# A two-layer hybrid decoder on one core: one input projection for prompt and samples, and a tile's expert choice moved to the next stretch

## The reference

```python
mod = (silu(c) @ w_ada + b_ada)                    # 6 x 1024 columns: shifts, gains, gates
h = rms_norm(x, norm1_g) * (1 + sc1) + sh1
qa, ka, va, qb, kb, vb, zb, bb, ab, qc, kc, vc = split_cols(h @ w_in, IN_SPLITS)   # 3592 columns
...                                                # three mixers: dilated windows, gated delta, sticks
x = x + gt1 * (concat([o_a, o_b, o_c]) @ w_out)
h2 = rms_norm(x, norm2_g) * (1 + sc2) + sh2
x = x + gt2 * peer_ffn(h2, peer_wq, peer_keys, peer_u, peer_v)
```

## The kernel before

| stretch | us in the trace | prompt lane | sample lane | experts |
|---|---|---|---|---|
| A | 22 to 54 | 4 chunks of modulation, layer 0 | - | - |
| B | 56 to 992 | unit 0, with layer 1's modulation beside its two choices | layer 0, with the other 8 chunks of layer 0's modulation between `heads` and `delta_sample` | - |
| C | 992 to 1931 | unit 1 | - | samples of layer 0; unit 0 |
| D | 1936 to 2780 | unit 2 | - | unit 1 |
| E | 2784 to 3638 | unit 3 | - | unit 2 |
| F | 3643 to 4684 | - | layer 1 | unit 3; samples of layer 1 |

## Time and profile before

### The profile page before, as it was taken

How to read it: one execution, slowest core, us unless ns; L and a number is a source line. 1 busy time by engine, 2 the same in 40 slices (tenths; PEclk the granted TensorE clock), 3 DMA queues, 4 the chain that set the end, 5 groups by cost and what they waited for, 6 DMA issues and landing times. The chain is left out here.

```text
span 4692.3 us, 42307 instructions
## 1 busy us (share of the span) xinstructions
PE 3425.7 (73%) x11982; PEld 1910.2 (41%) x11982; DVE 2843.8 (61%) x5777; ACT 877.2 (19%) x2045; POOL 2587.5 (55%) x2244
## 2 busy tenths in 40 slices
PE   5966768539298889575887967498898436748897
PEld 2624543126154554262455426255553113213351
DVE  1225552556866648787774688868649767584322
ACT  1113110011142112112321211242221011000120
POOL 0000362025767757687774667777656767665563
PEclk8986789759589999796998988799999767869896
DMA  6451375549989989899998889999988989999995
GB/s 229 139 180 56 101 227 177 187 104 320 354 318 345 385 308 339 331 399 342 366 376 320 306 334 395 353 346 361 367 306 308 378 303 348 362 382 377 336 330 154
DMA packets 586674, 1401.71 MB, mean 299 GB/s; under 512 B 67314, under 2 KB 287659, under 8 KB 585244
## 3 DMA queue, kind: packets, MB, share of 16 engines
q0 software_dynamic: 306176, 1107.44, 63.6%
q1 hardware_dynamic: 261836, 274.77, 17.7%
q10 hardware_dynamic: 18432, 16.79, 1.1%
HBM read 1387.11 MB, written 11.88 MB: 298 GB/s over the span
## 5 line engine op out<-in xcount | busy, mean ns | idle before, releaser
L2496 PE MATMUL bank<-arena 128*128 128x512 f32 (+1 forms) x3264 | 1589.6, 636 | 200.5 <-PEq L2493 117.9
L2392 POOL DMA_INDIRECT arena<-in_peer_u_dram,arena x1056 | 1279.6, 1212 | 693.2 <-issue 303.1
L2392 POOL DMA_INDIRECT arena<-in_peer_v_dram,arena x1056 | 1160.5, 1099 | 749.2 <-PE bank L2496 448.4
L2442 DVE CUSTOM_DVE_ANT_0 arena<-arena 128x1024 f32<-128x1024 f32 (+1 forms) x1056 | 1269.8, 1224 | 447.5 <-DMA arena<-in_peer_u_dram,arena 417.4
L2496 PEld LDWEIGHTS bank<-arena 128*128 128x128 f32 (+1 forms) x3264 | 614.8, 196 | 1013.6 <-issue 869.5
L2479 ACT ACTIVATE arena<-arena 128x128 f32<-128x128 f32 (+1 forms) x816 | 301.5, 394 | 1072.9 <-PE bank L2496 686.1
L2458 DVE SCALAR_TENSOR_TENSOR arena<-arena 128x1024 f32<-128x1024 f32 x232 | 297.6, 1283 | 243.6 <-DMA arena<-in_peer_v_dram,arena 223.3
L799 PE MATMUL bank<-arena 128*128 128x256 f32 (+3 forms) x1472 | 368.9, 414 | 101.0 <-PEq L792 95.9
L2138 POOL DMA_INDIRECT arena<-in_cache_sb_k_dram,arena x64 | 84.0, 1312 | 550.4 <-POOLq L2131 530.2
L799 PEld LDWEIGHTS bank<-arena 128*128 128x128 f32 (+1 forms) x1472 | 247.0, 170 | 220.8 <-issue 156.1
L641 PE MATMUL bank<-arena 128*9 128x512 f32 x384 | 180.3, 627 | 66.9 <-PEq L637 45.9
(11 more groups left out here) (339 smaller groups left out, 3730.0 us busy)
## 6 DMA issues: line engine op xcount, KB each, us to landing
arena<-in_w_in_dram SPq DMA_DIRECT2D x78, 1024.0 KB, 13.2
arena<-in_w_ada_dram SPq DMA_DIRECT2D x24, 2048.0 KB, 8.4
arena<-in_w_out_dram SPq DMA_DIRECT2D x24, 1024.0 KB, 13.0
arena<-in_peer_wq_dram SPq DMA_DIRECT2D x24, 1024.0 KB, 15.0
arena<-in_peer_u_dram,arena POOLq DMA_INDIRECT x1056, 7.4
arena<-in_peer_v_dram,arena POOLq DMA_INDIRECT x1056, 6.2
arena<-in_cache_sb_k_dram SPq DMA_DIRECT2D x128, 128.0 KB
arena<-in_cache_sb_v_dram SPq DMA_DIRECT2D x128, 128.0 KB
```

The costliest lines, as they stand in the source:

```text
L2392: pool_.indirect_dma_start(G_[g % GR][0:b.parts, :], None, tables[0 if which == "u" else 1], bass.IndirectOffsetOnAxis(ap=b.index[:, n:n + ...
L2442: vec.tensor_tensor_reduce(row, row, b.h, 1.0, 0.0, ALU.mult, ALU.add, b.AV[0:b.parts, n:n + 1]).then_inc(freed_by_dve, 1)
L2496: last = pe_.matmul(ps[6 + i][0:b.rows, :], DG[owners[g][1] % NDG][0:b.parts, 0:b.rows], G_[g % GR][0:b.parts, i * GBLK:(i + 1) * GBLK], s ...
```

## The change

1. **One projection for both lanes.** In stretches B and E `project` also takes the 8 samples of that layer: their normed rows stand as 8 more columns of `HT`, so a feature matmul has 264 columns, and each of the other eight chunks gets one more group of 8 matmuls (`"sample"`). The sample units' own norm, `project` and loads of `w_in` are gone; `sample_norm` runs ahead of the projection (in E as a stage of the prompt lane). In E the sample's rows go through three staging buffers to DRAM (`ROWS`), and `rows_back` reads them at F's start. `delta_sample` gets features (`BF`) and transposes them back for `DB`.
2. **Order in B.** The sample lane begins with its norm, then the 8 chunks of modulation (0.02 to 0.25 of the stretch, beside the projection), then waits for the prompt's projection (`after_lane`) and goes on.
3. **Choice.** B's prompt lane ends with unit 0's first choice, with all 12 chunks of layer 1's modulation beside it (length 80 where the two choices had 59 each). The choice of unit 0's second tile runs in C, from 0 to 0.25 of it (`second_choice`).
4. **Stores of modulation.** SP no longer waits for a store; DVE does, two chunks later.
5. **Last phase v.** In F, phase v of tile b alone puts every second row on DVE (`ON_DVE_ALONE = 2`).
6. F's sample lane has 0 to 0.8 of the stretch (before 0.85).

```diff
 def on_dve(b, n):
-    return not b.sample and n >= FIRST_ON_DVE and n % ON_DVE == ON_DVE - 1
+    return not b.sample and n >= FIRST_ON_DVE and n % b.every == b.every - 1
...
-                                    sp_.dma_start(MODD[l][:, cols(n - 2)], MT[n % 2]).then_inc(stored, 16)
-                                    sp_.wait_ge(stored, 16).then_inc(stored, -16)
+                                    sp_.dma_start(MODD[l][:, cols(n - 2)], MT[n % 2]).then_inc(v_landed[n % 2], 16)
...
+                            if n >= 2:
+                                vec.wait_ge(v_landed[n % 2], 16).then_inc(v_landed[n % 2], -16)
...
-            def project(u, m):
+            def project(u, m, s=None):
...
-                        mine = [(c, kind, i) for i in range(nt)]
+                        mine = [(c, kind, i) for i in range(nt)] + ([(c, kind, "sample")] if s else [])
...
+                        if spill and t - 2 in of_samples:
+                            k = of_samples.index(t - 2)
+                            lo, hi, _ = CHUNKS[groups[t - 2][0]]
+                            sp_.wait_ge(act2sp, 1).then_inc(act2sp, -1)
+                            sp_.dma_start(ROWS[:, lo:hi], s.m.STAGE[k % 3][:, 0:hi - lo]).then_inc(k_landed[k % 3], 16)
...
+                                elif i == "sample":
+                                    last = pe_.matmul(ps[t % BANKS][0:NB, 0:hi - lo], m.HT[:, k, n_:wide],
+                                                      m.W[c % ring][:, k, 0:hi - lo], start=(k == 0), stop=(k == KD - 1))
...
+                                if out_to_dram and k >= 3:
+                                    act_.wait_ge(k_landed[k % 3], 16).then_inc(k_landed[k % 3], -16)
...
-                    return [paced(begin, 8), paced(project(u, m), 80), paced(heads(u, m), 14)] + between + [paced(delta_sample(u, m), 75),
+                    return [paced(heads(u, m), 14), paced(delta_sample(u, m), 80),
...
+                before = [paced(sample_norm(s.u, m, m.HT), 8)] if s is not None and s.normed is None else []
+                return before + [paced(begin, 14), paced(project(u, m, s), 120 if s else 102), ...
...
-                        paced(choose_tile(u, e, 0, meanwhile[0:1]), 59), paced(choose_tile(u, e, 1, meanwhile[1:2]), 59)]
+                        paced(choose_tile(u, e, 0, meanwhile), 80 if meanwhile else 59)] + \
+                       ([] if meanwhile else [paced(choose_tile(u, e, 1), 59)])
...
+                        b.every = ON_DVE_ALONE if last and len(phase) == 1 else ON_DVE
...
+        def second_choice(u, span):
+
+            ticks, programs = LC.choose_tile(u, None, 1)
+            return [span[0] + (span[1] - span[0]) * (n + 1) / ticks for n in range(ticks)], programs
...
-        late = [LP.modulate(1, tiles, GBLK, half * MOD // 2, (half + 1) * MOD // 2) for half in range(2)]
+        late = [LP.modulate(1, tiles, GBLK)]
...
+               [([paced(LS.sample_norm(samples[0], rooms[0][0], m.HT), 8)], 0.0, 0.02), ([paced(rest, 50)], 0.02, 0.25), (rest_of_samples, 0.255, 1.0)], [])
...
+            choice = second_choice(u, (0.0, 0.25)) if k == 0 else ([], {})
...
-                window([], LS.token_mixers(samples[1], (LAST_at, arena_cols)), phases + [[("u", s)], [("v", s)]], (0.0, 0.85))
+                of_sample = [paced(LS.rows_back(samples[1], rooms[1][0]), 4)] + LS.token_mixers(samples[1], rooms[1])
+                window([], [(of_sample, 0.0, 0.8)], phases + [[("u", s)], [("v", s)]], choice)
```

More of the change, by code:

```diff
@@ L745, in project @@
                 tap = {i: f for f, i in feature_at.items()}
-                BANKS = 2 if u.sample else 4
+                of_samples = [i for i, g in enumerate(groups) if g[2] == "sample"]
+                spill = s is not None and s.m.STAGE is not None
+                BANKS = 4
                 ring = len(m.W)
                 ticks = len(groups) + 3
-                T = None if u.sample else m.TMP
+                T = m.TMP
                 def destinations(g):
@@ L834, in dve @@
                     for t in range(ticks):
-                        if t == 0 and not u.sample:
+                        if t == 0:
                             if u.first:
@@ L1875, in dve @@
                 def dve():
-                    for t in range(ticks):
+                    for t in range(-ahead, ticks):
                         if t == 2:
@@ L2346, in build, with experts @@
             batches = 0
[L2349 removed]
+        def experts(phases, last=False):
             walked = []
```

164 lines of the change are left out of this document (114 added, 50 removed).

## The result

The changed kernel takes **4643.28 us** (median of 4 runs, 4635.06 to 4653.99) where the kernel before took 4711.81 in the same comparison: ratio 0.9856, 95% interval 0.9827 to 0.9885, some 68 us saved where 103 were forecast. A second comparison on another chip gave 0.9859 (0.9836 to 0.9883).

| us | before | forecast | after | difference |
|---|---|---|---|---|
| B | 936 | -55 | 890 | -46 |
| C | 944 | +28 | 976 | +32 |
| D | 848 | 0 | 844 | -4 |
| E | 859 | +6 | 893 | +34 |
| F | 1041 | -82 | 966 | -75 |

A forecast was written before the change was run, and what follows sets the result against it. B was held to be bound by chains of waits, C, E and F by bytes and gathers in flight. Terms -55 (B), +28 (C), +6 (E), -82 (F) summed to -103, from median 4713.41 to 4610 us; range 4500 to 4685.

The forecast's parts named there:

- B, -55 forecast: Stretch B: projection and modulation -25, middle +20, end -50 us; bounds carried 0 and -110.
- -25, +20, -50: B's parts: fewer matmul records; samples' stick stage put ahead of the first choice; end keeping only samples' tail and modulation.
- the bound of 60: B's middle: samples' stick stage moved ahead of the first choice adds at most 60 us; +20 taken.
- C, +28 forecast: Stretch C: moved choice of 60 us, 18 hidden, 42 between tile a's dots, 14 absorbed; bounds 0 and +60.
- rival 2: C and F's third phase: POOL cannot issue gathers while DVE works beside them; C loses 60 us; 4667 us; chance 0.04.
- E, +6 forecast: Stretch E: samples' norm and 128 records join the first phase, whose length gathers set; bounds 0 and +44 us.
- F, -82 forecast: Stretch F: first phase -55, second +13, third -40 us; bounds -17 and -109.
- Rival 1: B: samples' chain of 659 us, as long and begun as late as before, keeps B's length; 4665 us; chance 0.17.
- Rival 3: E: ACT waits five times for stores to `ROWS` behind loads of `w_in`, 228 us; 4832 us; chance 0.05.
- Rival 4: Whole kernel, all goes well: B -110, C and E 0, F -109; 4494 us; chance 0.11.
- Rival 5: C: the choice comes late, tile b's gathers wait on POOL, C pays 35 us more; 4645 us; chance 0.06.

The follow-up runs named there:

- the square: Four kernels by projections and choice's place; B: 936 us before, 926 choice alone moved to C, 932 changed kernel with choice back in B, 890 both.
- e7_no_sample_groups: Changed kernel, E without the samples' eight row groups, their copies and stores; F reads rows of w_in instead: 4638.83 us, ratio 0.9838 to the kernel before.
- e11_f_samples_later: Changed kernel, F's sample lane from 0.07 to 0.9 of the stretch instead of 0 to 0.8: 4626.87 us, ratio 0.9826 to the kernel before.
- e4_b_samples_sooner: Changed kernel, B's sample lane behind the projection ends at 0.92 of the stretch instead of 1.0: 4632.86 us, ratio 0.9833 to the kernel before.
- e10_choice_first: Changed kernel, moved choice from 0 to 0.05 of C instead of 0 to 0.25: 4638.14 us, ratio 0.9864 to the kernel before.

## Why the prediction was right, and where it was wrong

The direction held, and the time lies in the range. Made against the profiled executions, the sum forecast 4591 and the profile shows 4635, 44 us less saved: E makes 28 of them, B 9, F 7, C 4, and D gives 4 back. That it came within the range is in part luck: inside B and F the terms missed by more than the sums, in both directions.

*B, -55 forecast, -46 measured.* By parts -25, +20, -50 came out as -30, +43, -59, so the middle was sized too small: the part ahead of the first choice grew by 43, well on the way to the bound of 60, and the end gave more. By the square the middle's 43 us go with the moved choice alone: with the choice back in B the first choice stood 31 us ahead of its old place, about as far as the beginning had become shorter. And the parts were added as if each had a price of its own. That holds up to the first choice; but the end became 27 us longer with the projection and 53 shorter with the choice, and 59 shorter with both. So one projection saves 4 us of B, and the choice 10. The working was near for the sum of the two and would have been far off for either.

*C, +28 forecast, +32 measured* (30 to 32 of it before tile a's last dot). The path is in the main the one that the step named, gathers that wait for buffers which the dots free; that the gathers themselves take longer (rival 2, below) it left out. The choice is 52 us of DVE here, not 60; 37 of them fell between the dots, where the step had 42, and they cost 32, nearly all, where the step let free time take a third. The step took its place in C as given; 0.1 instead of 0.25 makes it 11 to 18.

*E, +6 forecast, +34 measured: the step that failed.* It said that the gathers set the length, since PE had free time. The sample groups cost 9 to 13 us all the same (`e7_no_sample_groups`), though PE is busy for 61% of that phase: the gathers waited 20.0 us for the dots, and 3.4 without the groups. The longer lengths cost 6 us in the third phase and give them back in the first. Some 10 us of the second phase stay open: it lies at 401 to 425 us after, at 400 and 410 in the two profiles with E's code of before, and no run tells these apart. By the same two profiles E before is 859 and 872 us, so that of the +34 some 21 to 34 are the kernel's.

*F, -82 forecast, -75 measured*, but each phase otherwise: -18 for -55, -26 for +13, and up to the tail -30 between the marks used here, where -40 was forecast. The first phase lost the loads of `w_in` and took up other loads and 29 us of DVE; the step counted what goes and not what moves up when the sample lane has a stage less. The third gave some 10 us for the rows on DVE, and the other 20 otherwise: the step set the gathers' pace at 1.28 us, from 50 us at 401 GB/s; with PE waiting for rows the phase ran at a DMA share of 0.98 and 358 GB/s, 201/128 = 1.57 us a gather. The sum came within 7 us because misses of 37, 39 and 10 us cancel. That F's phases share the same bytes may be why (`e11_f_samples_later` moved 26 us from one to another), but it is argued and not shown, and no run gives the samples their own projection back in F.

**The rivals.** Rival 1, the samples' chain: it took 945.3 - 295.8 = 649 us, nearly the old 659, and B became shorter by about as much as the chain began earlier. That looked like it, and `e4_b_samples_sooner` speaks against it: the chain ended 50 us sooner, and B was as long. Nor is its length fixed: 599 us there, 686 with the choice back in B.

Rival 2, POOL held by DVE, would by its size have cost C 60 us; C paid 31 and, with the same DVE work in another place, 11 to 18. But its sign is there: the median gather of `peer_u` beside tile a's dots takes 1157 ns on POOL, and 1038 before. All gathers of `peer_u` in C's beginning, before:

```profile
L2392 POOL DMA_INDIRECT arena<-in_peer_u_dram,arena x148 | 183.1, 1237 | 309.6 <-POOLq L2387 234.3 <-issue 37.2 <-PE bank L2496 20.5
```

In the changed kernel:

```profile
L2471 POOL DMA_INDIRECT arena<-in_peer_u_dram,arena x148 | 197.7, 1336 | 315.6 <-POOLq L2466 221.5 <-DVE arena L2521 37.8 <-issue 35.9
```

With the choice at 0.1:

```profile
L2471 POOL DMA_INDIRECT arena<-in_peer_u_dram,arena x148 | 185.5, 1253 | 317.1 <-POOLq L2466 225.0 <-issue 36.6 <-DVE arena L2521 35.0
```

So C's price has two parts: gathers start later, behind the dots (37.8 us, where it was 17.6 before), and they take longer on POOL (197.7 us instead of 183.1). The second part follows the place of the choice and not DVE's share (69, 78 and 83% of 316, 347 and 327 us): tile a's 128 gathers took 158 to 161 us in the three profiles with no choice, or 2 us of it, beside the dots, 170 to 176 in the eight with 0.25, 161 to 168 in the three with 0.1.

What makes a gather longer can be read from the timeline. Here are two gathers of the kernel before, one beside a row of phase v on DVE, one beside the choice (start, duration):

```profile
2640.61 1.28 DVE L2458 SCALAR_TENSOR_TENSOR arena<-arena 128x1024 f32<-128x1024 f32 x1
2640.83 1.87 POOL L2392 DMA_INDIRECT arena<-in_peer_v_dram,arena  x1 [0.31 <-issue]
...
2643.00 0.94 POOL L2392 DMA_INDIRECT arena<-in_peer_v_dram,arena  x1 [0.30 <-issue]
2643.05 0.28 DVE L324 FIND_INDEX8 arena<-arena 128x8 uint32<-128x128 f32 x1
```

The first ends at 2642.70, 0.81 us after the row's end. So it is throughout: in the changed kernel 620 gathers began with 0.13 us or more of a dot still to run, and the median one ended 0.81 us after that dot (the middle half 0.810 to 0.814); 167 began beside the choice's searches (MAX8, FIND_INDEX8, MATCH_REPLACE8 and the load of their values) and took 0.89 to 0.94 us. Dots and rows read two tensors in SBUF, these searches one. So the searches don't hold a gather, as the earlier trace rows say, but the dots do, and between bursts of choice a gather begins beside a dot with more of it still to run: such gathers of tile a took 1.73 us in the mean, 1.45 before. By the Trainium skill, SBUF — State Buffer, section "Who interferes with whom", a DVE instruction with two inputs in SBUF contends with a GpSimd instruction that reads SBUF, as a gather reads its indices there. The trace agrees; where the prediction says that it does not, it set the page's lock against the choice, whose searches have one input. Rival 2 had part of the mechanism, then, and not its size.

Rival 3, the stores to `ROWS`: E grew by 34, not by 228, and ACT's waits at the plain rows were 40.1 us in E's first phase, 43.1 before. Rival 4 needed E and C at nothing. Rival 5 has no sign: the moved choice ended at 1238 us, and tile b's first gather stood at 1283.

## What to carry to other kernels

Where two lanes meet at the end of a stretch, shortening one can expose the other: price the pair of edits as a square of four kernels, since here 4 and 10 made 46. Work that is moved beside a full stretch should stand where its engine still waits; the same choice cost 31, 11 to 18 or 25 us by place alone. And where a lane is shifted within a stretch, time can move from one phase to another (26 us for 26 in `e11_f_samples_later`), so forecast the sum too.

## What the runs showed of the hardware that was not expected

A gather that POOL starts while DVE works on a dot or a row ends 0.81 us after that instruction (93 of 100 such gathers beside a dot ended 0.80 to 0.83 us after it), so that it takes up to 1.99 us where it takes 0.94 alone; the max and index searches of the choice don't lengthen it. The 2,112 gathers of the changed kernel took POOL 2461 us, some 480 more than at 0.94 each.

A phase that is nearly all gathers didn't reach the rate that 50 us of it showed: F's third phase, with PE waiting for rows, ran at a DMA share of 0.98 and 358 GB/s, where the slice of 401 GB/s had a share of 1.01. Executions of the same program differ by up to 53 us (`e10_choice_first`, 4619.5 to 4672.7), while B repeats within 9 us and C's beginning within 2; E's second phase alone moved by 24 us between kernels with the same code for E.
